# Sample tokens sent to their experts first in a one-core streaming encoder step: 96 of 128 gathered rows used ahead of the dense loop, 320 dense tokens instead of 384

## What is computed

```python
h = rmsnorm(x);  z = h @ w_in
fo = softmax attention, 8 heads of 64, causal, with forget bias c[t]-c[s]    # FoX
mo = softmax attention, 8 heads, latent keys and values, rotary part          # MLA
x = x + concat(fo, mo) @ w_o
# PEER, for each token t and each of 8 heads, h2 = rmsnorm(x):
q = h2 @ w_pq, normalised;  s1, s2 = q_half @ sub_keys        # 128 scores each
v1,i1 = top_k(s1,16); v2,i2 = top_k(s2,16); sv,si = top_k(v1+v2, 16)
e = i1[si//16]*128 + i2[si%16];  g = softmax(sv)               # 8*16 = 128 experts of 16384
a = peer_u[e] . h2;  x += sum(gelu(a) * g * peer_v[e])
y = rmsnorm_final(x)
```

## Time and profile before

| | |
|---|---|
| median of 3 runs | 2064.83 us (2064.49 to 2077.03) |
| profiled execution | 2057.58 us, span of the core 2055.7 us |
| mean granted clock of TensorE | 0.933 |
| busy, share of the span | PE 91%, PEld 74%, DVE 76%, POOL 44%, ACT 38% |
| DMA | 502.54 MB, mean 244 GB/s over the span |

### The profile page before, as it was taken

How to read it: one execution, slowest core, us unless ns; L and a number is a source line. 1 busy time by engine, 2 the same in 40 slices (tenths; PEclk the granted TensorE clock), 3 DMA queues, 4 the chain that set the end, 5 groups by cost and what they waited for, 6 DMA issues and landing times.

```text
span 2055.7 us, 28703 instructions
## 1 busy us (share of the span) xinstructions
PE 1875.9 (91%) x9135; PEld 1519.7 (74%) x9135; DVE 1565.2 (76%) x3265; ACT 779.7 (38%) x1298; POOL 913.9 (44%) x727
## 2 busy tenths in 40 slices
PE   6999999999989952665799999999999999999998
PEld 4883666664555642664799999999999999999997
DVE  4314333332267989996799999999999999999999
ACT  4322432220211112995344344443444344443443
POOL 0011000000004445001477777777777777777772
PEclk8999877779999875999999999999999999999999
DMA  6110212102111002445899999999999999999994
GB/s 235 42 61 0 82 55 112 52 1 114 41 41 42 21 1 80 176 181 205 327 415 407 397 408 405 409 403 399 414 413 397 394 399 417 416 392 413 405 413 194
DMA packets 159300, 502.54 MB, mean 244 GB/s; under 512 B 17776, under 2 KB 51504, under 8 KB 155536
## 3 DMA queue, kind: packets, MB, share of 16 engines
q0 software_dynamic: 73728, 268.47, 32.7%
q1 hardware_dynamic: 85520, 233.42, 29.5%
HBM read 470.99 MB, written 30.84 MB: 244 GB/s over the span
## 4 chain that ended last, share of the span: by engine, by line
PE 84%; DVE 12%; ACT 2%; issue 1%; DMA 1%; SPq 0%; DVEq 0%; ACTq 0%
PE ps L1117 25%; PE ps L1133 9%; PE ps L1134 9%; PE ps L1135 9%; PE ps L1036 6%; DVE asel L1417 4%; PE ps L1012 3%; PE ps L966 3%; DVE bsel L1409 3%; PE ps L854 2%; PE ps L855 2%; PE ps L856 2%; PE ps L920 2%; PE ps L982 2%; PE ps L952 2%; PE ps L1043 1%
## 5 line engine op out<-in xcount | busy, mean ns | idle before, releaser
L543 POOL DMA_INDIRECT vbuf<-in_peer_v,ix x256 | 381.0, 1488 | 221.6 <-DMA gate_matrix<-stage 143.9
L543 POOL DMA_INDIRECT ubuf<-in_peer_u,ix x256 | 383.3, 1497 | 156.0 <-POOL ix L598 108.9
L1133 PE MATMUL ps<-hh,uh 128*128 128x384 f32 x1024 | 346.2, 338 | 10.7 <-DVE ul L1158 10.7
L1134 PE MATMUL ps<-hl,uh 128*128 128x384 f32 x1024 | 345.0, 337 | 0.0
L1135 PE MATMUL ps<-hh,ul 128*128 128x384 f32 x1024 | 344.8, 337 | 0.0
L1441 DVE SCALAR_TENSOR_TENSOR ubuf<-ubuf,h 128x1024 f32<-128x1024 f32 x256 | 302.2, 1217 | 1.1 <-issue 1.1
L1117 PE MATMUL ps<-vh,acth 128*128 128x512 f32 x774 | 238.5, 389 | 0.0
L1117 PE MATMUL ps<-vl,acth 128*128 128x512 f32 x774 | 238.3, 389 | 0.0
L1117 PE MATMUL ps<-vh,actl 128*128 128x512 f32 x774 | 238.3, 389 | 0.0
L800 ACT ACTIVATE vh<-vb 128x1024 fp32r<-128x1024 f32 x128 | 136.1, 1063 | 242.9 <-PE ps L1117 242.7
L1133 PEld LDWEIGHTS ps<-hh,uh 128*128 128x128 f32 x1024 | 193.2, 189 | 16.2 <-DVE ul L1158 11.1
(11 more groups left out here) (289 smaller groups left out, 3049.7 us busy)
## 6 DMA issues: line engine op xcount, KB each, us to landing
ub<-in_peer_uT SPq DMA_DIRECT2D x129, 512.0 KB, 6.9
vb<-in_peer_v SPq DMA_DIRECT2D x128, 512.0 KB, 6.9
gate_matrix<-stage SPq DMA_DIRECT2D x12, 2048.0 KB, 6.3
gbuf<-gate_matrix SPq DMA_DIRECT2D x64, 384.0 KB, 11.2
wpq<-in_wpq SPq DMA_DIRECT2D x8, 1024.0 KB, 4.9
kTs<-in_past_k SPq DMA_DIRECT2D x8, 512.0 KB, 4.2
vs<-in_past_v SPq DMA_DIRECT2D x8, 512.0 KB, 4.9
w_o<-in_w_o SPq DMA_DIRECT2D x1, 4096.0 KB, 12.8
```

The source lines that it names most:

```text
L543: nc.gpsimd.indirect_dma_start(out=dst[:, slot, e, :], out_offset=None, in_=t_in[table], in_offset=bass.IndirectOffsetOnAxis(ix[:, slot, e ...
L1133: mm(ps[:, 6 + slot, 0:NTD], uh[:, slot, k], hh[:, k], start=(k == 0), stop=False)
L1134: mm(ps[:, 6 + slot, 0:NTD], uh[:, slot, k], hl[:, k], start=False, stop=False)
```

## The change

- **Order of the front.** The attention list holds three FoX units of the prompt, then the 16 sample units with one prompt unit after every two, then the other FoX units; the prompt's latent queries and MLA units follow behind `FIRST`. Between the FoX units that follow the last sample unit, the sample tile gets its output projection, norm, product-key queries and scores (`S_UP` to `S_SQUARE`), in one PSUM bank; its top-k is cut in pieces (a Python generator) that DVE takes four at a time in an attention iteration, five at a time in a latent query head, and the rest in one go.
- **Early rows.** With its experts known, the sample tile's first 96 of 128 experts are gathered into a ring of eight rows, u first, then v: 192 rows. DVE uses one in each iteration of the MLA attention, nine in each tile of the second norm, what is left of the 96 u rows after it, 12 v rows behind each of three head pairs, and the last 60 ahead of the gate matrix. The other 32 experts of the samples go into the loop.
- **Top-k** of the prompt takes four tiles, eight rows a sort; queries of a head now precede the scores of the head before.
- **Dense tokens** are tiles 0 and 1 and half of tile 2: 320. The other 64 tokens of tile 2 sit twice on the 128 partitions, each copy with 64 of the 128 experts (their hidden rows and choices are moved by small DMAs), so they take 64 steps of one row. Gate matrix: 10 chunks of 32 tokens instead of 12.
- **Loop:** a step has a row of tile 3, and a second one of the half tile (steps 0 and 2 of four) or of the samples (step 3); step 1 has no second row. The half tile's values use one matmul for high and low part together (`half_pair`, 128 stationary columns of 64 + 64). At the end the two halves are added by PE (`pairs`).
- Addresses in SBUF are laid out anew, and w_o, w_pq and the sub-keys are loaded twice, for the samples and for the prompt.

The core of the diff (names of tensors and semaphores of the moved stages left out):

```diff
-TD = 3
-NTD = TD * P
-TG = T - TD
+NTD = 320
+HT = 64
+EARLY = 96
+RING = 8
+TURNS = BLOCKS // STEPS
-QUERY_ORDER = [("queries", 0), ("scores", 0), ("queries", 1), ("scores", 1)] + [
-    (step, h + n) for h in range(2, PH, 2) for step in ("queries", "scores") for n in range(2)]
+QUERY_ORDER = [("queries", 0)] + [x for h in range(1, PH) for x in (("queries", h), ("scores", h - 1))] + [("scores", PH - 1)]
+PLAN = [("prompt", m) for m in range(3)]
+for k in range(SAMPLES):
+    PLAN.append(("sample", k))
+    if k % 2 and k < SAMPLES - 1:
+        PLAN.append(("prompt", 3 + k // 2))
+SAMPLE_END = len(PLAN) - 1
+PLAN += [("prompt", m) for m in range(3 + SAMPLES // 2 - 1, FOX_UNITS)]
+FIRST = len(PLAN)
+PLAN += [("prompt", m) for m in range(FOX_UNITS, FOX_UNITS + MLA_UNITS)]
...
+        def rows_in_step(s):
+            return GROUP if s != 1 else 1
+        ROWS4 = 2 * EARLY
+        IN_STEP, IN_TILE, IN_PAIR = 1, 9, 12
+        USED_AT = [EARLY + pair * IN_PAIR for pair in range(PH // 2)]
...
 GpSimd
+            def early_rows(limit):
+                for q in range(issued[0], min(limit, ROWS4)):
+                    if q >= RING:
+                        pool.wait_ge(row_used, q - RING + 1)
+                    j = q % EARLY
+                    nc.gpsimd.indirect_dma_start(
+                        out=ring[:, q % RING, :], out_offset=None, in_=t_in["peer_u" if q < EARLY else "peer_v"],
+                        in_offset=bass.IndirectOffsetOnAxis(eidx4[:, j:j + 1], 0), ...
+            for pair in range(PH // 2):
+                early_rows(USED_AT[pair] + RING)
+                decode(2 * pair + 3, top.onehot2, top.i16f[:, :, :, 1, :], head_rows(e2, pair))
+                if pair < PH // 2 - 1:
+                    decode(2 * pair + 4, top.onehot, top.i16f[:, :, :, 0, :], head_rows(e1, pair))
+            early_rows(ROWS4)
...
 PE
+                for n, v in enumerate((vh[:, s % 2], vl[s][:])):
+                    for half in range(2):
+                        ins = mm(ps[:, 4 + half], half_pair[:, s % 2], v[:, half * 512:(half + 1) * 512], ...
+                for d in range(2):
+                    ins = tile_pair(d)
...
 DVE
+            for n_ in range(FIRST + 4):
+                attend(n_, 0, FIRST)
...
+                if n_ >= S_TOPK:
+                    choose(4)
+            for h in range(MH):
...
+                choose(5)
+            choose(200)
+            for n_ in range(FIRST, ALL + 4):
+                attend(n_, FIRST, ALL)
+                early_rows(IN_STEP)
...
+                early_rows(IN_TILE)
+            early_rows(EARLY - taken[0])
+            for pair in range(PH // 2):
...
+                if pair < PH // 2 - 1:
+                    early_rows(IN_PAIR)
...
+            early_rows(ROWS4)
             dve.wait_ge(selT_copied, 3)
```

More of the change, by code:

```diff
@@ new lines, in _ @@
+            act.wait_ge(dense_done, 1)
+            A(both[:], ps[:, 4:6].rearrange("p a b -> p (a b)"), ACT.Copy).then_inc(both_ready, 1)
+            for u, t in enumerate(LAST_ORDER):
+                if t in (3, TS):
+                    act.wait_ge(ss3_ready, u + 1)
+                else:
+                    if t < 2:
+                        act.wait_ge(dense_done, t + 2)
+                        rows = ps[:, 2 * t:2 * t + 2]
+                    else:
+                        act.wait_ge(both_done, 1)
+                        rows = ps[:, 6:8]
+                    link(A(yout[:, t], rows.rearrange("p a b -> p (a b)"), ACT.Square, accum_out=small[:, 40 + t:41 + t]))
@@ L990, in _ @@
+            for n in range(FIRST + 3):
+                if n < FIRST:
                     scores(n)
[L991 removed]
+                if 2 <= n < FIRST + 2:
                     transpose_probabilities(n - 2)
@@ L1003, in project_out @@
+            for n in range(FIRST, ALL + 3):
+                if n < ALL:
+                    scores(n)
+                if FIRST + 2 <= n < ALL + 2:
+                    transpose_probabilities(n - 2)
+                if n >= FIRST + 3:
+                    values(n - 3)
             def project_out(t):
                 if t == 0:
-                    pe.wait_ge(wo_loaded, 16)
+                    pe.wait_ge(wo_loaded, 48)
                     pe.wait_ge(o_copied, 8)
-                    pe.wait_ge(lat_copied, 1)
@@ L1076, in _ @@
             for step, h in QUERY_ORDER:
-                if (step, h) != ("queries", 0):
-                    {"queries": queries, "scores": key_scores}[step](h)
+                {"queries": queries, "scores": key_scores}[step](h)
             pe.wait_ge(sc_copied, PH)
@@ L1143, in _ @@
             values_block(PER - 1, dense_done, last_block=True)
+            pe.wait_ge(acc_done, BLOCKS + PER)
+            pe.wait_ge(ga_ready, BLOCKS + 2)
+            for half in range(2):
+                mm(ps[:, 6 + half], pairs[:, 0:P], x2[:, 2, half * 512:(half + 1) * 512], start=True, stop=False)
+            pe.wait_ge(both_ready, 1)
+            for half in range(2):
+                last = mm(ps[:, 6 + half], pairs[:, HT:HT + P], both[:, half * 512:(half + 1) * 512], start=False, stop=True)
+            last.then_inc(both_done, 1)
         @block.vector
@@ new lines, in first_keys @@
+            def first_keys(x, ready, choices):
+                dve.wait_ge(onehot_ready, ready)
+                one = flat(x.onehot)
+                link(V.tensor_tensor(one, one, x.i16f[:, :, :, 0, :].rearrange("p s t k -> p (s t) k").unsqueeze(2)
+                                     .broadcast_to(square), ALU.mult))
+                yield
+                for s in range(2):
+                    ins = V.tensor_reduce(choices[s], x.onehot[:, s], AX.X, ALU.add)
+                link(ins)
+                yield
```

1312 lines of the change are left out of this document (771 added, 541 removed).

## The result

The changed kernel takes 2218.86 us (median of 4 runs, 2213.66 to 2219.91) beside 2065.51 us: a ratio of 1.0724, 95% interval 1.0682 to 1.0766. It is slower, as forecast (2190, own bounds 2125 to 2255). The profiled execution took 2219.80 us, with a span of 2218.0 and a mean granted clock of 0.87 instead of 0.93.

A forecast was written before the change was run, and what follows sets the result against it. In the loop PE, DVE and DMA were all taken as nearly full. Gate matrix ending at 1198, opening 28, loop 940 and end 18 gave a span of 2184, stated as 2190 us; own bounds 2125 to 2255, range 2075 to 2270.

The forecast's parts named there:

- Rival (b): Loop: DMA holds a step at 7.7 us (395 GB/s), +38, about 2230 us; chance 0.12.
- (c): Loop: uneven rows not evened out, each group of four at the two-row step, 7.83 us: +55, 2245 us; chance 0.05.
- Term (2): Front, sample attention: a batch's cache load waits for the values two batches before; 5.5 us bare, 33 us for six batches.
- Rival (d): Attention: 512-column sample matmuls lift the clock from 0.77 towards 1.0, up to 59 us less: 2130 us; chance 0.10.
- Term (4): Front: sample choices not interleaved stand in DVE's program ahead of the prompt's latent attention, and PE stops: 28 us.
- The wait for cumulative sums: Front: scores 0 waits for twelve DVE operations behind the samples' rotation, about 8 us with semaphores.
- the ring of eight and the decodes before the next gather: Top-k, behind pairs: POOL runs eight rows ahead, then decodes twice before gathering; twelfth row used after 30.4 us, not 14.4.
- the mutual blocking: Top-k: two-input DVE rows and POOL's decode block each other, up to 9 us a pair, 27 in all; outside the sum.
- The 28 us: Opening of the loop: 28 us instead of 35.6, as eight late value gathers go out earlier.
- Rival (a): Front: run-ahead of PE and POOL's ring hides loads, drain and rows; 2028 us; chance 0.11 faster, 0.07 within 1%.

## Why the prediction was right, and where it was not

- **Span.** The forecast was a slower kernel, by waits and rows in front that a shorter loop does not pay for, and so it came. 2184 forecast, 2218.0 measured. By stage, forecast and measured: first top-k at 728, 733.7; top-k and rows behind pairs 250, 266.1; tail 96.5, 101.8; gate matrix 123, 122.0; opening 28, 38.4; loop 940, 943.4; end 18, 12.6. All but the gate matrix and the end ran long, the top-k stage by most, 16 us.
- **Loop.** 7.4 us a step was the forecast, 7.404 the measurement; PE 7.15, measured 7.185; DVE's steps 7.83 and 5.49, measured 7.83 and 5.48. Rival (b), 7.7, is refuted, and so is (c), 7.83: the uneven rows are evened out. The value of 7.4 was chosen between two rates of DMA; the experiments show that DMA and DVE shared it. That it fits to 0.004 us is luck.
- **Front.** The sum fits within 6 us, but its parts do not, so that is partly luck. Term (2), loads: 33 forecast, 18.8 of waits, and 18 more by the clock, which the forecast had as 5 for all gaps. Rival (d) looked for the clock to rise from 0.77; it was 0.70 in the stretch with the samples, and 0.75 over all attention. Term (4), the drain: 28 forecast, and 5 for the first row; 39 measured for both, since the samples' own decode lies between them. Only 12 us could be taken by moving choices. The wait for cumulative sums: 8 forecast, 5.5 measured.
- **Top-k.** The forecast's reason was the ring of eight and the decodes before the next gather: 30.4 us for twelve rows. They took 37.7 behind the first pair (772.0 to 809.7) and 37.4 behind the others. The term that was mis-sized is the end of the two decodes, 20 us after DVE's one-hots in the sum. That is right without rows beside them (19.1) and 7 short with them (26.0): a single decode takes 9.5 us in the kernel with gathers ahead (796.86 to 806.4) and 14.1 beside rows (769.98 to 784.07). So the step that failed is the one left out of the sum, the mutual blocking. It was named as "up to 9 us a pair, 27 in all" and cost the stage 7 a pair, 21 in all. On DVE's side alone it is larger, since eight rows take 21 to 25 us beside the decodes and 11.3 without; most of that lies where DVE would have waited for the ring, so DVE stands idle for 7 us behind a pair and not for some 15. The Trainium skill, "SBUF — State Buffer", section "SBUF: two separate sides", calls the shared port pair an exclusive lock for a whole instruction; this trace agrees, with POOL's multiply 4.54 us beside top-k and 6.49 beside DVE's one-hots, and DVE's small product and rows of up to 4.58 and 5.5 us. The pairs themselves were cheaper than forecast (38.4 instead of 39.8), which hid 6 us of it.
- **Tail.** 79 us were forecast for 60 rows, at POOL's pace; they took 84.9. It was nearly the right number for the wrong engine: POOL can issue every 1.31 us, and it is DVE's chain of accumulations, 1.41 a row, that sets the pace. Eight rows that lie in the ring beforehand, with POOL only gathering, go no faster (11.22 us).
- **Opening.** The 28 us were mis-sized by 10, of which 4 are where the window was cut: from ACT's last copy of gates to the first matmul of u it is 34.2 us (1225.83 to 1260.02), against 35.6 before (957.51 to 993.12). The forecast took some 10 us of late gathers out of the way of the first value block. On the chain of waits that block's transfer takes 7.58 us instead of 9.10, so what the gathers took there was small. No run took the rest apart.
- **Rival (a)**, waits covered: 2028. The kernel without any rows, which leaves work out, reaches 2001, so 218 us hang on the rows: it is their work on DVE that nothing covers. All waits that the experiments could remove came to 92 us, not to the 153 that were lost.

## What to carry to other kernels

Work moved off a balanced loop must land where its engine has free time: 192 rows of 1.2 to 1.4 us on DVE cost 218 us in front, and the loop that they made room for gave 104. Before moving two-input work on DVE next to GpSimd's element-wise work, ask which runs while the other does; putting POOL's DMA issues in that place instead gained 60 us here with one line. And a short repeated wait of PE should be priced with the clock that it takes from the work around it: here 15 us of waits cost 33.

## What the runs showed of the hardware

- DVE with two SBUF operands and POOL's tensor-tensor operations held each other up for whole instructions: a 128x96 product on DVE took 4.58 us instead of 0.25 beside POOL's multiply, and that multiply 6.49 instead of 4.54. DVE's top-k operations (one SBUF operand) ran beside the same decode without loss on DVE's side: 275 to 285 ns for each maximum, search and replacement, with the decode and without.
- Idle times of 2 to 4 us, 22 to 25 us apart, came with a granted clock of 0.50 to 0.59 over 120 us in which PE was 79 to 86% busy; 3.7 us of such waits in all came with 0.54 to 0.69, and a run without the loads' traffic with 0.58 to 0.69.
- Gathers and plain loads together moved 418 GB/s for 850 us (the loop without DVE's part of the samples' row). The Trainium skill, "DMA: Bandwidth & Descriptors", Specifications, gives a core's share of HBM as about 358 GB/s; with one core running, here as in the kernel before, the trace shows more, and the measurement decides.
